# Decay levels of a gated recurrence, multiplied block by block: 32 (level 7: 64) tokens instead of 128

## The reference, cut to what matters

```python
b = jnp.cumsum(gc, axis=2)                                   # gc: log of the forget gate
diff = b[:, :, :, None, :] - b[:, :, None, :, :]
decay = jnp.exp(jnp.minimum(diff, 0.0)) * tri[:, :, None]
A = jnp.einsum('bhtsd,bhsd->bhts', qc[:, :, :, None, :] * decay, kc)
o = (jnp.einsum('bhts,bhsv->bhtv', A, vc)
     + jnp.einsum('bhtd,bhdv->bhtv', qc * jnp.exp(b), state))
```

## Time and profile before

| what | value |
|---|---|
| time, median of 3 runs | 1457.23 us (1456.3 to 1458.39) |
| profiled execution, span | 1455.4 us |
| PE busy | 1312.6 us, 90%, 4936 matmuls |
| PE weight load busy | 829.2 us, 57% |
| DVE busy | 815.5 us, 56% |
| ACT busy | 412.4 us, 28% |
| POOL busy | 647.9 us, 45% |
| L805 (levels), matmul | x480, 58.4 us, 275 ns each |
| chain that ended last | PE 63%, DMA 23%, DVE 7% |

### The profile page before, as it was taken

One profiled execution on the slowest core, in us unless ns is written; L12 is line 12 of the kernel. 1 busy time (PEld: TensorE's weight loads), 2 busy tenths in 40 slices (PEclk: granted clock), 3 DMA queues, 4 the chain that ended last, 5 costly groups with the idle time before them and its releaser, 6 DMA issues.

```text
span 1455.4 us, 14776 instructions
## 1 busy us (share of the span) xinstructions
PE 1312.6 (90%) x4936; PEld 829.2 (57%) x4936; DVE 815.5 (56%) x1680; ACT 412.4 (28%) x1032; POOL 647.9 (45%) x643
## 2 busy tenths in 40 slices
PE   9999999999999999999998989967877787778886
PEld 8888687747888687747656646533333332323332
DVE  0775377431465367443237775879887654544555
ACT  0532244211332244112232332322313232122123
POOL 0556667331546667331202434454544454544440
PEclk9999999999999999999999999988989899999999
DMA  9544334345443334357255999999999999999995
GB/s 375 189 160 174 116 152 172 133 184 199 187 161 158 132 143 176 116 202 257 69 231 232 377 413 409 421 420 419 420 419 421 419 420 420 420 420 420 420 420 211
DMA packets 53734, 407.71 MB, mean 280 GB/s; under 512 B 6150, under 2 KB 8731, under 8 KB 11035
## 3 DMA queue, kind: packets, MB, share of 16 engines
q0 software_dynamic: 36864, 268.45, 44.7%
q1 hardware_dynamic: 15706, 137.28, 24.2%
q10 hardware_dynamic: 1088, 1.05, 0.4%
HBM read 404.63 MB, written 1.07 MB: 279 GB/s over the span
## 4 chain that ended last, share of the span: by engine, by line
PE 63%; DMA 23%; DVE 7%; issue 3%; ACT 2%; POOL 1%; ACTq 0%; POOLq 0%; DVEq 0%
PE pj L665 23%; DMA ring<-in_peer_uv,vM 10%; PE bank L1087 10%; PE pj L701 9%; PE pj L680 7%; DMA yT<-in_peer_uv,vM 5%; PE bank L805 3%; DMA more_rows<-in_peer_uv,vM 3%; DMA qvE<-in_peer_uv,vM 2%; PE pj L957 2%; DMA hv<-in_peer_uv,vM 2%; DMA qM<-in_peer_uv,vM 1%; PE bank L638 1%; PE bank L907 1%; DVE tri L1841 1%
## 5 line engine op out<-in xcount | busy, mean ns | idle before, releaser
L665 PE MATMUL pj<-xT,ring 128*128 128x256 f32 (+2 forms) x1536 | 324.3, 371 | 1.8 <-ACTq L1135 1.7
L665 PEld LDWEIGHTS pj<-xT,ring 128*128 128x128 f32 (+1 forms) x1536 | 277.7, 189 | 42.4 <-issue 2.7
L592 POOL TENSOR_SCALAR more_rows<-more_rows,lbt 128x256 f32<-128x256 f32 x168 | 178.4, 1062 | 16.4
L626 POOL DMA_INDIRECT ring<-in_peer_uv,vM x101 | 120.1, 1189 | 116.5 <-PE bank L1087 104.4
L590 POOL TENSOR_SCALAR mod_part<-more_rows,lbt 128x256 f32<-128x256 f32 x24 | 26.1, 1088 | 271.2 <-issue 120.0
L701 PE MATMUL pj<-ring,yT 128*128 128x512 f32 x320 | 140.3, 594 | 0.0
L1305 ACT ACTIVATE rope<-vM 128x4 f32<-128x4 f32 (+3 forms) x84 | 17.1, 204 | 408.0 <-DVE big L1841 325.2
L593 POOL TENSOR_TENSOR mod_part<-mod_part,more_rows 128x256 f32<-128x256 f32 x168 | 126.5, 753 | 14.0
L1087 PE MATMUL bank<-ring,causal 128*128 128x512 f32 x200 | 99.3, 635 | 17.4 <-ACT causal L1313 17.4
L1087 PE MATMUL bank<-ring,tri 128*128 128x512 f32 x204 | 97.6, 618 | 16.5 <-ACT tri L1313 16.5
L701 PEld LDWEIGHTS pj<-ring,yT 128*128 128x128 f32 x320 | 59.9, 190 | 71.1 <-issue 71.1
(11 more groups left out here) (366 smaller groups left out, 2146.3 us busy)
## 6 DMA issues: line engine op xcount, KB each, us to landing
ring<-in_units SPq DMA_DIRECT2D x44, 2048.0 KB, 9.3
more_rows<-in_w_ada SPq DMA_DIRECT2D x24, 1024.0 KB, 4.8
ring<-in_units SPq DMA_DIRECT2D x2, 1536.0 KB, 6.5
ring<-in_peer_uv,vM POOLq DMA_INDIRECT x101, 23.2
memT<-in_mem SPq DMA_DIRECT2D x1, 1024.0 KB, 5.4
ring<-in_units SPq DMA_DIRECT2D x2, 512.0 KB, 6.6
ring<-in_units SPq DMA_DIRECT2D x1, 1024.0 KB, 9.0
xT<-in_x_turned SPq DMA_DIRECT2D x1, 1024.0 KB, 10.8
```

Source lines behind the costliest of these rows:

```text
L592: do(g.tensor_scalar(mod_w[:, c, :], mod_w[:, c, :], silu_c[:, c:c + 1], None, ALU.mult))
L626: pool.indirect_dma_start(row_slot[k], None, d["peer_uv_2"], bass.IndirectOffsetOnAxis(ap=expert[:, t, j:j + 1], axis=0))\
L665: ins = nc.tensor.matmul(pj[s][0:n, 2 * m + first:2 * m + stop], ring[:, slot, at:at + n], act[:, c, first:stop], start=(c == 0), stop=(c ...
```

## The change

Levels 1 to 7 multiply only the blocks of a tile that can hold pairs of the level. `level_blocks(m)` lists them as (first key token, first query token, size). For levels 1 to 5 these are the four diagonal blocks of 32; for level 6 the blocks with keys 0 to 31 and queries 32 to 63, and keys 64 to 95 and queries 96 to 127; for level 7 keys 0 to 63 and queries 64 to 127. A block's keys are its 32 (64) weight columns, its output lies on the partitions of these keys, and it streams 32 (64) query columns. Level 8 is as before. Of a bank the parts outside the blocks now hold whatever was there, so level 1 too is copied through `level_mask`, whose first level now includes the diagonal, and `tri` is set to zero once at the start. The matrix `near` and its load are gone.

Products at L805: 240 before, 4 x (5 x 32 + 16 + 8 + 4) = 752 after.

```diff
--- before.py
+++ after.py
@@ -143,6 +143,14 @@
 UNIT = {key: n for n, key in enumerate(STREAM)}
 
 
+def level_blocks(m):
+
+    half = 2 ** (m - 1)
+    if half < 32:
+        return [(k, k, 32) for k in range(0, P, 32)]
+    return [(k, k + half, half) for k in range(0, P, 2 * half)]
+
+
 def big_uses():
 
     out, uses, turn = {}, [0, 0], 0
@@ -253,6 +261,7 @@
         h = 2 ** (m - 1)
         same = (i[:, None] // (2 * h)) == (i[None, :] // (2 * h))
         level[:, m - 1] = same & ((i[:, None] // h) % 2 == 0) & ((i[None, :] // h) % 2 == 1)
+    level[:, 0] |= np.eye(P, dtype=np.int32)
     t = np.arange(T)
     causal = np.where(t[None, :] <= t[:, None], 0.0, NEG_BIG).astype(np.float32)
     rot = np.zeros((P, 33), np.float32)
@@ -273,7 +282,6 @@
     return {
         "c_eye": np.eye(P, dtype=np.float32),
         "c_level": level.reshape(P, 7 * P),
-        "c_near": ((i[:, None] == i[None, :]) | ((i[:, None] % 2 == 0) & (i[None, :] == i[:, None] + 1))).astype(np.float32),
         "c_causal": causal, "c_rot": rot,
         "c_inv_freq": np.tile(inv, P // 16).reshape(1, P).astype(np.float32),
         "c_bias0": np.ascontiguousarray(bias[:P, :, :P]).astype(np.float32).reshape(P, HEADS2 * P),
@@ -303,7 +311,6 @@
         eye = sb("eye", [P, P])
         ones_mean = sb("ones_mean", [P, P])
         rot = sb("rot", [P, 33])
-        near = sb("near", [P, P])
         level_mask = sb("level_mask", [P, 7, P], u8)
         causal = sb("causal", [P, TT, T])
         vec = sb("vec", [P, 104])
@@ -480,7 +487,7 @@
         V_LB, V_OUT, V_QN, V_KN, V_INV = 0, 16, 18, 22, 24
         V_C, V_POOL, V_N1, V_N2, V_BADA = 25, 33, 37, 45, 53
         N_B2 = 5
-        N_CONST = 15
+        N_CONST = 14
 
         block = ctx.enter_context(nc.Block())
 
@@ -524,7 +531,6 @@
             load(vec_rows[V_N2:V_N2 + 8, :], d["norm2_g_2"].rearrange("l (h p) -> (l h) p", p=P))
             load(vec_rows[V_BADA:V_BADA + 48, :], d["b_ada_2"].rearrange("l (h p) -> (l h) p", p=P))
             load(rot[:, :], d["c_rot"])
-            load(near[:, :], d["c_near"])
             load(flat_b[:, 800:1696].bitcast(i32), d["c_level"])
             load(causal[:, :, :], d["c_causal"].rearrange("(a p) s -> p a s", p=P))
             load(flat_b[:, 0:T].bitcast(i32), d["positions"].to_broadcast([P, T]))
@@ -798,11 +804,13 @@
                     B = bank_of(key)
                     for n in range(4):
                         if m == 8:
-                            k, q = K[:, n, 0:P], Q[:, n, P:T]
-                        else:
-                            hd, t = (4 * j + n) // TT, (4 * j + n) % TT
-                            k, q = K[:, hd, t * P:(t + 1) * P], Q[:, hd, t * P:(t + 1) * P]
-                        ins = nc.tensor.matmul(B[:, n * P:(n + 1) * P], k, q, start=True, stop=True)
+                            ins = nc.tensor.matmul(B[:, n * P:(n + 1) * P], K[:, n, 0:P], Q[:, n, P:T], start=True, stop=True)
+                            continue
+                        hd, t = (4 * j + n) // TT, (4 * j + n) % TT
+                        for k0, q0, size in level_blocks(m):
+                            ins = nc.tensor.matmul(B[k0:k0 + size, n * P + q0:n * P + q0 + size],
+                                                   K[:, hd, t * P + k0:t * P + k0 + size],
+                                                   Q[:, hd, t * P + q0:t * P + q0 + size], start=True, stop=True)
                     last(ins)
 
             def readout(l, n):
@@ -1426,6 +1434,7 @@
             do = steps(dve, "dve_step")
             do(v.memset(vec_rows, 0.0), "vec_zeroed")
             do(v.memset(ones_mean[:, :], 1.0 / P), "ones_ready")
+            do(v.memset(flat_tri, 0.0))
             do(v.memset(eps[:, 0:1], RMS_EPS))
             do(v.memset(eps[:, 1:2], LN_EPS))
             bank_filled(dve, (0, ("VEC",)))
@@ -1617,10 +1626,7 @@
                             B = bank_of(key)[:, :].rearrange("p (h k t) -> p h k t", k=TT, t=P)
                             dst = tri[:, 2 * j:2 * j + 2, 0:3:2, :]
                             square = [P, 2, TT, P]
-                            if m == 1:
-                                mask = near[:, :].unsqueeze(1).unsqueeze(1).to_broadcast(square)
-                                do(v.tensor_tensor(dst, B, mask, ALU.mult), *bank_free(key))
-                            elif m < 8:
+                            if m < 8:
                                 mask = level_mask[:, m - 1, :].unsqueeze(1).unsqueeze(1).to_broadcast(square)
                                 do(v.copy_predicated(dst, mask, B), *bank_free(key))
                             else:
```

## The result

| | before | changed |
|---|---|---|
| median, us | 1456.76 (1455.39 to 1458.39, 4 runs) | 1447.67 (1446.79 to 1450.41, 4 runs) |
| profiled span, us | 1455.4 | 1448.6 |
| PE busy, matmuls | 1312.6, 4936 | 1296.5, 5960 |
| DVE busy | 815.5 | 814.1 |
| POOL busy | 647.9 | 643.4 |

The ratio is 0.9938, 95% interval 0.9926 to 0.995: about 9 us faster, where 17 were forecast. The profiled execution of the changed kernel is the slowest of its four, 6.8 us shorter than that of before. I look for the missing part from the level outwards.

The account below looks back on a forecast made before the run. TensorE bounds the two layers, the gather the expert stage behind them. Of TensorE's 24.9 us, 0.7 + 6.2 + 1.2 + 0.4 = 8.5 a layer are kept, 17 in all: 1455.4 - 17 + 1.8 = 1440.2, about 1440 us; range 1431 to 1456.

Parts of the forecast that it names:

- the main case: Whole kernel, case (c): 1440 us, its own range from 1434 to 1449; chance 0.68.
- a change of width: TensorE entering and leaving narrow passes: the engine drains, 0.33 us for the two changes, charged to each shortened level.
- The level: TensorE, levels 1 to 5: 16 slots x 0.031 = 0.50, plus 0.33, makes 0.83 us against 1.78.
- a pair seen in one call: L785 before the change: passes on two partition groups start some 0.01 us apart, at one's pace; carried over to four.
- Kept where TensorE has other work: Levels outside the places of waits, per layer: 6.2 us kept, plus 1.2 of 1.9 at second group's levels 3 and 4.
- The other edits: Level 1's predicated copy 0.1 us showing at most, memset nothing behind VectorE's idle, one load less under 0.2 us gained.
- Kept at the places of waits: Where VectorE is full, per layer: first group's levels 1, 2 keep 0.7 of 1.9 us; second's 5 to 7, 0.4 of 2.4.
- (a): Rival: all of TensorE's 24.9 us arrive, since VectorE and ScalarE mostly follow TensorE: 1432 us; chance 0.08.
- (b): Rival: 32-column passes start one after another, 0.031 us apart, whatever partitions they write; 2.31 us a level, 1464; chance 0.11.
- (b'): Rival: as (b), with starts 0.018 to 0.026 us apart on TensorE: 1449 to 1457 us; chance 0.13.
- GpSimd's pieces: Modulation pieces TensorE takes: slack 2.0 to 2.5 us; if they don't shift with levels 1 and 2, each layer loses 2.
- The instruction stream: TensorE: 512 more products, 2,048 instructions; between nothing and 8 us of stalls at 28 levels, taken as nothing.

Follow-up runs that it names:

- the kernel with one group: Changed kernel, but every block writes output partitions 0 to 31 (level 7: 0 to 63): 1462.25 us.
- the blocks three times: Changed kernel with the blocks of levels 1, 2 (first group) and 5, 6 (second) multiplied three times, level 7 twice: 1469.4 us.
- blocks only there: Changed kernel with blocks only at levels 1, 2 of the first group and 5 to 7 of the second, others 128x128x128: 1457.72 us.
- half the products: Changed kernel with levels 1, 2 (first group) and 5 to 7 (second) at full width, two of each bank's four products: 1444.39 us.
- the first three orders: Changed kernel with TensorE's list reordered, cumulatively: projections moved into the waits 1444.77 us, two modulation products moved too 1439.1, Y7 between G1a and G1b too 1437.83.
- the last order: Third reordered kernel, with level 16 behind the output product's first half, the sum before both, VectorE reading the sum after level 15: 1431.46 us.
- the first order: Changed kernel with GMa ahead of S2 and P0, Y0 behind GMb, and O0's first tile between levels 6 and 7 of the second group: 1444.77 us.

## Why the prediction was half right

Forecast 1440, measured 1447.67: inside the range, in the direction given, with 9 of the 17 us. That it is inside owes something to luck: the main case reached down to 1449 for a change of width at twice the price or for late pieces of GpSimd, and neither is what took the 8 us.

**The level, right.** 0.83 us forecast, 0.89 to 0.90 measured. The 64 passes take 0.60 us (0.57 between the first and the last start, 0.03 for the last), not 0.50, and the two changes of width 0.29, not 0.33. Level 7 of the first group takes 166.76 to 167.79, 1.03 us, less than the 1.26 forecast: in front of it stands Y4, whose products have 64 weight columns as well, so it doesn't pay both changes, which the forecast had charged it. For the four groups together TensorE saves 24 x 0.88 + 4 x 0.75 = 24.1 us, forecast 24.9. That a pair seen in one call carries over to four groups for 64 passes was the bold step, and it held; the kernel with one group shows that nothing else makes the gain of levels 1 to 5.

**Kept where TensorE has other work, right.** 14.8 us forecast for the 18 levels, 13.2 by the end of the second layer's levels, and a median 13.9 to 14.5 us better than before, in the kernel that keeps full width at the places of waits. The other edits cost nothing, as forecast.

**Kept at the places of waits, wrong.** The forecast had +0.7 and +0.4 a layer, +2.2 in all; blocks there make the kernel slower: by 3.2 us where all other levels are in blocks too (1446.42 against 1443.26), and by 0.6, which is within the noise, where no others are (1457.72 against 1457.17). The waits themselves I had seen coming, and 0.7 us at S2 was even their right size. What the sum lacks is a term for the clock behind them. A dip is worth 3.4/2 = 1.7 us where TensorE has work: S2 starts 0.76 us earlier and ends no earlier; Y9, the sum and the output product take 16.80 us (262.37 to 279.17), where before has 15.04 (269.09 to 284.13), 1.76 more. That is how an edit that only removes work from an engine at a place where the engine can't use it can come out negative.

**The sum from place to place.** By the start of level 18, 284.13 before and 279.17 after, layer 1 has won 5.0 us; by that of the second layer, 613.23 and 603.16, 10.1. The forecast was 8.5 and 17. Of the 3.5 us missing in the first the places of waits explain 2.8: 1.1 was forecast of them, and by the rows they bring -0.3 (the projection behind Y0 starts at 106.39, before at 106.10) and -1.4 (6.35 us ahead at level 15, 4.96 at level 18). The other 0.8 is what the kernel with blocks everywhere else lacks as well (13.2 of 14.8 in two layers): 0.06 us at each of its levels, and Y7's wait of 0.9, of which I had allowed 0.7. Behind the layers 10.1 shrinks to 6.8 in the profiled execution. 1.3 us go at 662, where a dip follows a wait of 2.9 us that was there before, without a dip (8.8 ahead by 701.66, before 710.44). Another 0.7 go at 771.2, where a dip lasts 6.8 us and that of before, at 782.4, 3.4 (8.1 ahead by 779.93, before 787.98). The last 1.2 go in the gather's stage, which I haven't traced. The other three runs are 2.2 to 3.6 us faster than the profiled one.

**The cause of the dips, not settled in full.** I counted over the profiles of all kernels but the one with the blocks three times. At the levels of the two layers TensorE has 22 waits of 1.3 to 2.4 us (four each in the changed kernel, its repeat, blocks only there and half the products; two each in the first three orders), and 12 of them have a dip behind them. No dip lies there without such a wait: none in the trace of before, none in the kernels with full width at these places or everywhere, none with one partition group, none in the last order. The longer the wait, the more often: 4 of the 10 waits of 1.3 to 1.6 us, 6 of the 10 of 2.0 to 2.1, and both of 2.4, with dips of twice the length. So an estimate from these counts is 4 x 12/22 x 1.7 = 3.7 us for the changed kernel's four waits, against the forecast's gain of 2.2: a loss of 1.5, where the two pairs of kernels measured 3.2 and 0.6. That speaks for the waits, and the passes of full width with a dip show that the narrow ones aren't needed. Against a rule that simple: a wait of 1.73 us at about 345 us, before a projection, has no dip behind it in any of these profiles, and that of 2.9 us at the end of the second layer has one in 9 of 13, but not in the trace of before and, as the kernel with full width everywhere has it too, not by the blocks' doing. In the kernel left out of the count, where TensorE runs out of instructions, one dip (161.3 us) follows a wait of only 1.2 us, which in the first order no dip followed. What besides the length of the wait decides, and whether the lighter load of narrow passes has a part in it, stays open.

**The rivals.** (a), 1432, everything kept, fell for this kernel, but it is what the last order reaches with the same products: 24.3 us against TensorE's 24.1. What that order alone does to the kernel before was not run; TensorE's waits there sum to little. (b) and (b') fell: starts in different partition groups come 1 to 8 ns apart within their fours and pairs. The Trainium skill's page TensorE: Matmul & The Clock Gate, section "Wait — 56ns, not 53.3ns?", has starts never under about 25 ns; the trace agrees within a partition group (31 to 32 ns, for columns of fp32) and not across groups, where four start every 32 to 34 ns for a whole level. GpSimd's pieces, put at 2 us a layer, cost the changed kernel nothing in the first layer and 0.56 us in the second (a sum at 475.13), and took 3.6 a layer once the waits in front of them were gone. The instruction stream, put at 0 to 8 us, took nothing that shows, and 18 us with three times the passes in a row.

## What to carry to other kernels

Time taken off the busiest engine counts only where its next task isn't already waiting for someone; at the other places leave the slow form or, better, move a long independent task into the new wait, and look for the next cover each time: here VectorE, then GpSimd, then a bank, for 15 us in all. When new waits of one to three microseconds appear on TensorE, read its granted clock in the stretches behind them, since these can cost more than the waits. Small fp32 products whose outputs lie on different groups of 32 partitions are worth splitting, if the groups take turns and the change of width is paid once for many of them.

## What the runs showed of the hardware

- Four fp32 passes with 32 weight and 32 moving columns, on four groups of output partitions, run at the pace of one: four each 32 to 34 ns, 64 in 0.60 us. On one group they start 31 to 32 ns apart.
- Going to narrow weights and back costs about 0.3 us: 0.89 - 0.60 = 0.29 for a level, 2.34 - 64 x 0.0317 = 0.31 on one group, 0.33 in the earlier trace rows for the pair of 64.
- TensorE's granted clock fell to 0.50 for 3.4 us behind waits of 1.3 to 2.9 us in some executions and not in others, and for 6.8 us behind the two waits of 2.4: 12 times behind the 22 waits of 1.3 to 2.4 us at the levels, and there never without one, in all kernels but the one with the blocks three times.
- TensorE can run out of instructions: 191 passes of 32 columns in 1.8 us, then 6.47 us of standing still until packets of 16 KB had come. With 64 or 96 such passes in a row, at about the same pace, it didn't happen. Why the packets came late isn't shown.
